# A dense tile of expert gates: placed by indirect accumulating writes instead of one-hot products

## The reference

```python
q = (xt @ w_q).reshape(T, PEER_HEADS, 2, PEER_DK_HALF)            # 8 heads
s = einsum('thpd,hpnd->thpn', q, sub_keys)                        # 2 x 128 key scores for each head
s1, i1 = top_k(s[:, :, 0], 16);  s2, i2 = top_k(s[:, :, 1], 16)
cand = s1[..., :, None] + s2[..., None, :]                        # 256 candidates, top 16 of them
top_s, pos = top_k(cand, 16)
idx = i1 * 128 + i2 at pos                                        # one of 16384 experts
gates = softmax(top_s)
a = gelu(u_table[idx] . x) * gates                                # for each token 8 x 16 experts
y = sum over the 128 chosen experts of a * v_table[idx]
return rms_norm(h + y)
```

## Time and profile before

| | us |
|---|---|
| median of 3 runs | 1683.61 |
| lowest and highest | 1681.93, 1683.74 |
| the profiled execution | 1682.5 |
| its span | 1680.7 |
| TensorE busy | 1667.5 (99%) |
| VectorE busy | 1231.8 (73%) |
| ScalarE busy | 779.7 (46%) |
| GpSimd busy | 772.8 (46%) |

### The profile page before, as it was taken

How to read it: one execution, slowest core, us unless ns; L and a number is a source line. 1 busy time by engine, 2 the same in 40 slices (tenths; PEclk the granted TensorE clock), 3 DMA queues, 4 the chain that set the end, 5 groups by cost and what they waited for, 6 DMA issues and landing times.

```text
span 1680.7 us, 24604 instructions
## 1 busy us (share of the span) xinstructions
PE 1667.5 (99%) x9035; PEld 1471.1 (88%) x9035; DVE 1231.8 (73%) x2293; ACT 779.7 (46%) x1380; POOL 772.8 (46%) x484
## 2 busy tenths in 40 slices
PE   9999999999999999999999999999999999999998
PEld 6878877788888999999999999998888888888887
DVE  7877636744524699999999466744888888888886
ACT  6533326544212343456867767733343333333334
POOL 4544422344334778865555477775232223222220
PEclk9999999999999999999999999999999999999999
DMA  8322332374434889987878599997999999999993
GB/s 225 101 76 70 107 98 57 92 244 137 115 117 158 278 290 334 334 278 274 296 255 305 212 378 384 392 369 243 376 373 348 374 348 370 357 356 366 355 359 123
DMA packets 258655, 433.68 MB, mean 258 GB/s; under 512 B 14752, under 2 KB 181920, under 8 KB 256872
## 3 DMA queue, kind: packets, MB, share of 16 engines
q1 hardware_dynamic: 202520, 249.11, 45.4%
q0 software_dynamic: 36864, 134.23, 20.9%
q10 hardware_dynamic: 19152, 48.77, 7.9%
HBM read 372.82 MB, written 59.24 MB: 257 GB/s over the span
## 4 chain that ended last, share of the span: by engine, by line
PE 58%; DVE 7%; issue 2%; ACT 1%; DMA 1%; POOL 0%; ACTq 0%; DVEq 0%; SPq 0%
PE bank L252 17%; PE bank L254 17%; PE bank L253 17%; PE bank L1802 5%; DVE lists L1575 1%; DVE rows L1296 1%; DVE slot L1624 1%; DVE lists L1613 1%; DVE lists L1619 0%; DVE top_i L1573 0%; DMA rows<-in_u_rows,expert 0%; DVE top_i L1585 0%; DVE pair_i L1585 0%; DVE pair_i L1573 0%; ACT hot L1478 0%
## 5 line engine op out<-in xcount | busy, mean ns | idle before, releaser
L247 POOL TENSOR_TENSOR spl_a<-raw,spl_a 128x1024 fp32r<-128x1024 f32 x170 | 409.4, 2410 | 327.2 <-ACT spl_a L243 324.2
L243 ACT ACTIVATE spl_a<-raw 128x1024 fp32r<-128x1024 f32 x295 | 311.9, 1059 | 378.3 <-PE bank L254 348.1
L252 PE MATMUL bank<-act,spl_a 128*128 128x384 f32 (+1 forms) x1216 | 425.6, 350 | 4.2 <-ACT gl L1458 2.4
L254 PE MATMUL bank<-act,spl_a 128*128 128x384 f32 (+1 forms) x1216 | 417.3, 343 | 0.0
L253 PE MATMUL bank<-act,spl_a 128*128 128x384 f32 (+1 forms) x1216 | 417.1, 343 | 0.0
L252 PE MATMUL bank<-spl_a,aws 128*128 128x512 f32 x768 | 299.0, 389 | 0.0
L253 PE MATMUL bank<-spl_a,aws 128*128 128x512 f32 x768 | 298.8, 389 | 0.0
L254 PE MATMUL bank<-spl_a,aws 128*128 128x512 f32 x768 | 298.8, 389 | 0.0
L1287 POOL DMA_INDIRECT rows<-in_v_tab,expert x128 | 135.2, 1056 | 343.4 <-DVE hot L1693 335.0
L252 PEld LDWEIGHTS bank<-act,spl_a 128*128 128x128 f32 x1216 | 228.5, 188 | 16.2 <-issue 5.3
L253 PEld LDWEIGHTS bank<-act,spl_a 128*128 128x128 f32 x1216 | 228.6, 188 | 7.5 <-issue 0.7
(11 more groups left out here) (321 smaller groups left out, 2373.2 us busy)
## 6 DMA issues: line engine op xcount, KB each, us to landing
raw<-in_u_t SPq DMA_DIRECT2D x128, 512.0 KB
raw<-in_v_tab SPq DMA_DIRECT2D x128, 512.0 KB
dense_gates<-mixbuf ACTq DMA_DIRECT2D x12, 2048.0 KB
mixbuf<-dense_gates SPq DMA_DIRECT2D x32, 768.0 KB
gelu_ux<-gl ACTq DMA_DIRECT2D x120, 192.0 KB
mixbuf<-gelu_ux SPq DMA_DIRECT2D x30, 768.0 KB
raw<-in_w_in SPq DMA_DIRECT2D x43, 512.0 KB
raw<-in_w_q SPq DMA_DIRECT2D x16, 512.0 KB
```

Source lines behind the costliest of these rows:

```text
L243: eng.activation(spl(n, 0, slice(0, W)), raw[:, s, :], ACT.Copy).then_inc(hi_done, 1)
L247: eng.tensor_tensor(spl(n, 1, slice(0, W)), raw[:, n % RAW, :], spl(n, 0, slice(0, W)).bitcast(F32), ALU.subtract).then_inc(lo_done, 1)
L252: nc.tensor.matmul(out, w_hi, x_hi, start=first, stop=False)
L254: return nc.tensor.matmul(out, w_lo, x_hi, start=False, stop=last)
```

## The change

Tile 0 of the dense tokens (entry 1 of `TILES`, hence `PLACED = 1`) leaves the one-hot path. Its gates are added straight into a table in DRAM, `placed_d`, of 128 x 16384 floats (8.4 MB), laid out as the V stage reads it.

- The table is cleared in the first half: GpSimd sets a buffer of 128 x 256 floats to zero, and ScalarE writes it with four DMAs of 2.1 MB in the first four steps of the query projection, and waits for them at the end of that half.
- VectorE works out, in `place_index`, for each token and each of its 128 slots the element of the table (seven small operations), when it normalises that tile.
- GpSimd issues 128 accumulating indirect DMAs (`put`), each of which adds one float for each of 128 tokens, in the steps of `PUT_AT` (41 to 96). Before every sixteenth it waits until all earlier ones have landed, since two heads may choose the same expert.
- 64 quads stay (32 fewer), in steps 74 to 116 instead of 49 to 113; 8 blocks of `dense_d` instead of 12. `mix_gates` loads from both tables.
- VectorE takes 28 low halves of the U stage from GpSimd (`VEC_UNIT`: units 44 to 102, mostly the even ones), at the places `VEC_PIECE` of its own list. `wait_lo` waits for the right semaphore.
- The first gathers are issued at step 3, not 6, and `PAIR_DOTS`, `PAIR_QUADS`, `EXP_AT`, `SLOTS_AT` and `GATHER_AT` are new lists.
- ScalarE no longer waits for iota and copies it at the start of the stage; VectorE copies it inside its first pair.

```diff
-NQUAD = DT // QUAD
+PLACED = 1
+DB = (DT - P) // TB
+NQUAD = (DT - P) // QUAD
+VEC_PIECE = [66, 68, 70, 73, 75, 78, 80, 83, 87, ... 123, 125, 127, 128, 129]
+VEC_UNIT = [44, 46, 48, 50, 52, 54, 56, 58, 62, 64, ... 94, 96, 100, 102]
...
+        def wait_lo(eng, n):
+            if n - U0 in VEC_UNIT:
+                eng.wait_ge(vec_lo, VEC_UNIT.index(n - U0) + 1)
+            else:
+                eng.wait_ge(lo_done, n + 1 - sum(m < n - U0 for m in VEC_UNIT))
...
                 for n in range(BR0, U0):
                     split_lo(pool, n + LEAD)
+                    if n == WO0:
+                        pool.wait_ge(h_ready, 1)
+                        pool.memset(blank[:, :], 0.0).then_inc(blank_ready, 1)
...
                         k = n - WQ0
+                        if k < 4:
+                            act_e.wait_ge(blank_ready, 1)
+                            part = placed_rows[:, k * NC * P // 4:(k + 1) * NC * P // 4]
+                            act_e.dma_start(part.rearrange("p (r x) -> p r x", x=2 * P),
+                                            blank[:, :].unsqueeze(1).to_broadcast([P, NC // 8, 2 * P])) \
+                                .then_inc(placed_zero, 16)
...
+                act_e.wait_ge(placed_zero, 64)
...
-            sp.dma_start(gates_in[:, half, :, :, :].rearrange("p b c t -> p b (c t)"),
+            sp.dma_start(gates_in[:, half, 0:4, :, :].rearrange("p b c t -> p (b c t)"),
+                         placed_rows[:, c * P:(c + 4) * P]).then_inc(mix_in[half], 16)
+            sp.dma_start(gates_in[:, half, 4:, :, :].rearrange("p b c t -> p b (c t)"),
                          dense_d[:, :, c * TB:(c + 4) * TB].rearrange("b p x -> p b x")) \
...
-            EXP_AT = [20, 41, 63, 85]
-            SLOTS_AT = [None, 43, 65, 91]
-            GATHER_AT = [6, 6, 6, 7, 7, 7, 8, 11, 12, ... 115, 115, 116, 116, 117]
-            PAIR_DOTS = [0, 2, 4, 4, 6, 6, 6, 6, 6, 4, 4, 4, 4, 4, 4, 4]
-            PAIR_QUADS = [0, 0, 0, 0, 0, 0, 0, 0, 0, 8, 8, 8, 8, 8, 8, 8]
+            EXP_AT = [18, 39, 66, 94]
+            SLOTS_AT = [None, None, 68, 97]
+            GATHER_AT = [3, 3, 3, 4, 4, 4, 5, 8, 9, ... 118, 119, 119, 120, 120]
+            PUT_AT = [41, 41, 42, 42, 42, 43, 44, 44, 44, 44, 45, ... 92, 93, 93, 94, 94, 96, 96]
+            PAIR_DOTS = [0, 2, 4, 4, 6, 6, 6, 6, 6, 6, 6, 6, 6, 5, 5, 5]
+            PAIR_QUADS = [0, 0, 0, 0, 0, 0, 0, 0, 0, 0, 0, 0, 0, 8, 10, 10]
...
+                        sp.wait_ge(placed_in, 16 * SLOTS)
...
+                def put(k):
+                    if k == 0:
+                        pool.wait_ge(tk_slots, PLACED + 1)
+                        pool.wait_ge(placed_zero, 64)
+                    elif k % TOPK == 0:
+                        pool.wait_ge(placed_in, 16 * k)
+                    pool.indirect_dma_start(out=placed_d[:, :],
+                                            out_offset=bass.IndirectOffsetOnAxis(ap=place[:, k:k + 1], axis=0),
+                                            in_=place_g[:, k:k + 1], in_offset=None, compute_op=ALU.add) \
+                        .then_inc(placed_in, 16)
                 for j in range(NC):
-                    split_lo(pool, U0 + LEAD + j)
+                    if LEAD + j not in VEC_UNIT:
+                        split_lo(pool, U0 + LEAD + j)
                     for g in range(len(GATHER_AT)):
                         if GATHER_AT[g] == j:
                             gather(pool, g)
+                    for k in range(SLOTS):
+                        if PUT_AT[k] == j:
+                            put(k)
...
-                act_e.wait_ge(iota_in, 16)
-                act_e.activation(iota, iota_f[:, :], ACT.Copy).then_inc(iota_ready, 1)
...
+                def low_part(piece):
+                    if piece in VEC_PIECE:
+                        n = U0 + VEC_UNIT[VEC_PIECE.index(piece)]
+                        dve.wait_ge(hi_done, n + 1)
+                        dve.tensor_tensor(spl(n, 1, slice(0, W)), raw[:, n % RAW, :],
+                                          spl(n, 0, slice(0, W)).bitcast(F32), ALU.subtract).then_inc(vec_lo, 1)
...
                     if m % 4 == 0 and m and x == 2:
                         normalise(m // 4 - 1)
+                    low_part(PIECES * m + x)
                     quads(share(PAIR_QUADS[m]))
...
+                    if m == 0:
+                        dve.wait_ge(iota_in, 16)
+                        mark(dve.tensor_copy(iota, iota_f[:, 0, :]))
+                        settle()
...
+                def place_index():
+                    row = slot[:, PLACED % 2, 0, :, :].rearrange("p h k -> p (h k)")
+                    chunk = slot[:, PLACED % 2, 1, :, :].rearrange("p h k -> p (h k)")
+                    mark(dve.tensor_copy(place[:, :], chunk))
+                    settle()
+                    mark(dve.tensor_scalar(place[:, :], place[:, :], 3, None, ALU.bitwise_and))
+                    settle()
+                    mark(dve.tensor_copy(place_g[:, :], place[:, :]))
...
+                    mark(dve.tensor_copy(place[:, :], row))
+                    settle()
...
-                for step in range(16):
-                    quads(2)
-                    dots(2 + step % 2)
+                for step in range(11):
+                    low_part(PIECES * NT * PH // 2 + step)
+                    quads(min(3, NQUAD - made[1]))
+                    dots(min(2 + step % 2, SLOTS - made[0]))
```

More of the change, by code:

```diff
@@ L97 @@
 ROWS = 6
-NQUAD = DT // QUAD
+PLACED = 1
+DB = (DT - P) // TB
+NQUAD = (DT - P) // QUAD
+VEC_PIECE = [66, 68, 70, 73, 75, 78, 80, 83, 87, 90, 93, 95, 98, 100, 102, 105, 108, 110, 111, 114, 116, 118, 120,
+             123, 125, 127, 128, 129]
+VEC_UNIT = [44, 46, 48, 50, 52, 54, 56, 58, 62, 64, 66, 68, 70, 72, 74, 76, 78, 80, 82, 84, 86, 88, 90, 92, 94, 96,
+            100, 102]
 HOTS = 4
@@ L160, in build @@
     gelu_d = nc.dram_tensor("gelu_ux", (NC, P, DT), F32, kind="Internal").ap()
-    dense_d = nc.dram_tensor("dense_gates", (DT // TB, P, NC * TB), F32, kind="Internal").ap()
+    dense_d = nc.dram_tensor("dense_gates", (DB, P, NC * TB), F32, kind="Internal").ap()
+    placed_d = nc.dram_tensor("placed_gates", (P * NC * P, 1), F32, kind="Internal").ap()
+    placed_rows = placed_d.rearrange("(p x) o -> p (x o)", p=P)
     outer = ExitStack()
@@ L213, in load_unit @@
             if n >= RAW:
-                sp.wait_ge(lo_done, n - RAW + 1)
+                wait_lo(sp, n - RAW)
             s = n % RAW
@@ L990, in build @@
             qt = sb(ctx, "qt", [P, 2, T])
+            blank = sb(ctx, "blank", [P, 2 * P])
+            blank_ready = sem("blank_ready")
             keys_in = sem("keys_in")
@@ L1312, in build @@
             expert_f = sb(ctx, "expert_f", [P, 2, TOPK])
-            slot_t = sb(ctx, "slot_t", [P, 3, DT])
-            iota_f = sb(ctx, "iota_f", [P, P])
+            slot_t = sb(ctx, "slot_t", [P, 3, DT - P])
+            place = sb(ctx, "place", [P, SLOTS], U32)
+            place_g = sb(ctx, "place_g", [P, SLOTS])
+            iota_f = sb(ctx, "iota_f", [P, 2, P])
             scb = sb(ctx, "scb", [P, PAIRS, 2, 2, NK])
@@ L1332, in build @@
             hot_ready, hotg_ready = sem("hot_ready"), sem("hotg_ready")
+            placed_in = sem("placed_in")
             quad_done = sem("quad_done")
@@ L1399, in _ @@
                     if j == GATES_MIX_AT[0]:
+                        sp.wait_ge(placed_in, 16 * SLOTS)
                         for half in range(2):
-                            sp.wait_ge(stage_stored[half], 16 * (DT // TB // 2))
+                            sp.wait_ge(stage_stored[half], 16 * (DB // 2))
                     for part_no in range(2):
@@ L1453, in _ @@
                         for half in range(2):
-                            act_e.wait_ge(stage_stored[half], 16 * (DT // TB // 2))
+                            act_e.wait_ge(stage_stored[half], 16 * (DB // 2))
                     if j >= 4 and not kept:
@@ L1641, in shift @@
                         .then_inc(tk_shift, 1)
+                def place_index():
[6 more added lines that the diff above has]
+                    mark(dve.tensor_copy(place_g[:, :], place[:, :]))
+                    mark(dve.scalar_tensor_tensor(out=row, in0=row, scalar=float(NC * P), in1=iota_f[:, 1, :],
+                                                  op0=ALU.mult, op1=ALU.add))
+                    settle()
+                    mark(dve.scalar_tensor_tensor(out=row, in0=chunk, scalar=float(P), in1=row,
+                                                  op0=ALU.mult, op1=ALU.add))
+                    settle()
+                    mark(dve.scalar_tensor_tensor(out=row, in0=place_g[:, :], scalar=float(TB - P), in1=row,
+                                                  op0=ALU.mult, op1=ALU.add))
+                    settle()
+                    mark(dve.tensor_copy(place[:, :], row))
+                    settle()
                 def normalise(i):
@@ L1649, in normalise @@
```

(24 more changed lines are left out.)

17 lines of the change are left out of this document (10 added, 7 removed), and 21 rows, old and new, of tables (GATHER_AT, PUT_AT, QUAD_AT).

## The result

| | before | changed kernel |
|---|---|---|
| median, us | 1682.8 (1681.9 to 1683.7) | 1767.1 (1762.4 to 1776.1) |
| ratio, 95% interval | | 1.0508 (1.0486 to 1.0530) |
| the profiled execution, its span | 1682.5, 1680.7 | 1762.4, 1760.6 |

What follows compares the result with a forecast made beforehand. TensorE, busy 99% of the span, was taken as the bound: 28.8 + 1.9 + 2.1 = 32.8 us less gives 1650.8, plus 3 us of small waits, 1654 us (1.8% faster); range 1647 to 1694.

Steps and rivals of the forecast that it cites:

- The quads: On TensorE, 32 fewer quads at 0.90 us each take 28.8 us off the engine that sets the end.
- the transposition: At j = 43, TensorE no longer waits for the placed tile's gates or transposes them: 1.9 us less.
- the first steps: At the U stage's start, TensorE's wait for ScalarE's first Gelu, behind iota, goes: 2.1 us less.
- So a put may cost 1.12 us of GpSimd's queue before TensorE waits at all: In steps 41 to 96, GpSimd's remaining time plus 8.9 us of free delay allow 128 puts of 1.12 us.
- I take 1.0: A put costs GpSimd 1.0 us, near a gather's own busy time, and TensorE doesn't wait.
- rival (b): Puts on GpSimd outgrow the gain: a loss from 1.38 us a put; 1699 us at 1.5, 1768 at 2.04; chance 0.20.
- The drains: Before every sixteenth put GpSimd waits until earlier ones have landed: 7 drains, taken at 1 us each.
- VectorE and GpSimd hold each other up: VectorE's low halves meet GpSimd's splits at the shared port: 9 us on VectorE, about as much on GpSimd at most.
- VectorE's order: In the U stage, VectorE's new list keeps step with the high halves, with 9 us between, ending near 938 us.
- the cleared table: Writing 8.4 MB of zeros in the first half costs nothing: 49 us at spare bandwidth, some 70 left.
- SP's queue: A second gate-load issue (0.37 us) and the wait for puts at j = 119 on SP cost nothing.
- The whole sum: In steps 41 to 96, GpSimd's splits 72.0, gathers 51.5 and puts 128 need 251.5 of 258.2 us.

Runs made afterwards that it cites:

- plain puts: The changed kernel with its puts as plain indirect writes, not accumulating: 1704.8 us, 1.0125.
- the first 64 puts: The changed kernel with only the first 64 of its 128 puts, which stand in steps 41 to 73: 1710.7 us, 1.0164.
- every second one: The changed kernel with every second of its 128 puts, in the steps of its list (41 to 96): 1661.2 us, 0.9863.
- the puts spread: The changed kernel with its 128 puts spread evenly over steps 41 to 118, not 41 to 96: 1765.2 us, 1.0484.
- the first steps alone: The kernel before with only the change's start (no iota wait on ScalarE, first seven gathers three steps earlier) and tile 0's transposition one step later: 1678.1 us, 0.9969.

## Why the prediction was wrong, step by step

- **The quads, the transposition, the first steps (32.8 us): right.** 1650.8 forecast for a kernel whose suppliers keep up, 1650.5 measured without puts, so the sum holds; its terms weren't tried one by one. In the changed kernel the first Gelu stands at 530.68 where it was at 533.99, 3.3 us earlier for the 2.1 taken, and the first dot at 553.45 (about 555 forecast).
- **"So a put may cost 1.12 us of GpSimd's queue before TensorE waits at all": right in kind.** The 258.2 us of these steps were 257.9. A put costs 1.89, and TensorE waits. Two things were missing from it. The 1.12 us took a gather at 1.12 too, and beside the puts and VectorE's low halves a gather costs 1.41 (1.44 with plain puts); by the sum this and the drains are the some 30 us that were missing for plain puts. And the room must be there where the puts are, as the first 64 puts against every second one show; for the full list this hardly matters, since GpSimd is busy without a break there.
- **"I take 1.0": this step failed.** It is 1.59 busy and 0.30 of idle before, in both parts wrong. The idle time doesn't come from the waits of a gather: fifteen puts of sixteen wait for nothing and have the same 0.30 us ahead of them. And the accumulation adds 0.58 us. Of the range that I had bounded from rows for the price, 0.93 to 2.04 us, the true value lay near the upper end; its price, 128 x 1.89 = 242 us, makes 72.0 + 51.5 + 242 = 365 us of work for 267 of room and lead, 98 us too late. I gave all of rival (b) 0.20, this end of it less, and cut it from the range, with an argument (GpSimd only describes the transfer) for which no row spoke. Rival (b) was the case that came: a loss from 1.38 us a put on. By its own sum 1.89 us give 1749, where 1767 was measured; the rest is in the last point.
- **The drains: right in the changed kernel**, 5.4 us in 3 waits for the 7 taken. They grew to 14.2 us with plain puts, 16.9 with the puts spread and 10.8 with every second put.
- **VectorE and GpSimd hold each other up: right in kind, too small in size on VectorE.** See below: 20.7 us on VectorE where I had 9. TensorE waited for none of VectorE's low halves. On GpSimd it is 8 us in the gathers (1178 ns with VectorE's low halves, 1002 without, 46 times), about what I had put there; but they stand in the queue that TensorE waits for, so here they cost time. Without puts they cost nothing.
- **VectorE's order, the cleared table, SP's queue: right for this kernel.** TensorE's waits are for GpSimd's splits; VectorE's waits for quads grew to 76.6 us since TensorE is late, which is a consequence. The clearing DMAs landed in 11.4 us (median). The first Gelu of the stage stands at 530.68 with them, and at 530.13 in the kernel with the first steps alone, which clears nothing: 0.6 us between the two.
- **The whole sum.** The prediction's own terms with the measured price give 98 us of lateness. The 46 gathers cost 1.41 us where 1.12 was taken, 13 us, and the drains are 5: 116, where 113.9 were measured at step 100. The same sum gives 51.3 for plain puts, where 52.3 were measured. So it holds for two prices of the put. What a gather costs was read from the same traces, and no run tried the gathers' part by itself.

## What to carry to other kernels

An engine that is half idle over the span can be full in the only stretch where it is needed. Before work is moved to it, sum its queue for that stretch, with the idle time before each instruction counted as work, and for what stands there already too, as its price can rise beside the new work. Place the room step by step, since a queue in order can't use room that comes later. Where the price of the new operation is unknown and the sum turns from a gain to a loss within its bounds, the chance of loss is that of the price, and the range must hold its far end. One run of that operation by itself would have shown the price.

## What the runs showed of the hardware that was not expected

- An accumulating indirect DMA occupies GpSimd for 1.55 us at 128 rows and 1.41 at 64, a plain one for 0.97 and 0.90. In the traces with puts, 0.30 us of idle stand before each that follows another, also where it waits for no semaphore. One float for each row is described no faster than 4096 bytes for each row (0.96 us).
- VectorE's low half, which has two SBUF inputs, waits out a GpSimd split, and GpSimd's next indirect DMA then waits out the low half. This is the changed kernel's timeline:

```profile
790.89 2.89 POOL L264 TENSOR_TENSOR spl_a<-raw,spl_a 128x1024 fp32r<-128x1024 f32 x1
791.33 3.55 DVE L1612 TENSOR_TENSOR spl_a<-raw,spl_a 128x1024 fp32r<-128x1024 f32 x1 [12.07 <-ACT spl_a L260]
...
793.95 1.80 POOL L1318 DMA_INDIRECT rows<-in_u_rows,expert  x1 [0.17 <-issue]
```

The low half on VectorE starts at 791.33, and ends 1.10 us after the split (793.78), so nearly all its work is done after it. The gather that starts then lasts 1.80 us, 0.84 more than its median, and ends 0.87 us after VectorE is through (at 794.88), about its own price later. It is no single case: of the 50 gathers from 700 to 1092 us 12 last over 1.1 us, and each of them begins while such a low half is running; without low halves on VectorE none of 46 is longer than 1.02 us. A dot, whose second input is in PSUM, does not do this: in the kernel before 28 gathers began beside one, and the longest took 0.96 us. The 28 low halves took 55.0 us in all, 20.7 more than 28 x 1.225; the longest took 4.5 us. In the kernel without puts it was 36.9 us, 2.6 more. The Trainium skill, "SBUF — State Buffer", section "Who interferes with whom", says that an operation with two SBUF inputs is in the way of a GpSimd instruction that reads SBUF. The split that VectorE waited out agrees with it (3.55 us for 1.22). For the description of a DMA the same section infers that such an operation does not hold it up; the 12 gathers beside low halves speak against that, for an indirect DMA at least.
